# A fused two-block transformer kernel: 27 of the later modulation row chunks moved from TensorE to GpSimd, with one product with ones for each vector, and x loaded twice

## The chip, the cores and the metric

The kernel runs on one core of a Trainium2 chip. The metric is the device time of one execution in microseconds (us). Lower is better.

## What is computed

Two blocks follow each other on x (one sequence of 256 tokens, 2048 features, float32). The first has an RWKV-7 mixer beside a pooling mixer, the second has a short convolution beside banded attention, and both end in a gated convolutional feed-forward part. Only the modulation of the first block and what surrounds it matters here:

```python
c_act = jax.nn.silu(c)                      # c: 2048 numbers
mod = c_act @ w_ada[l] + b_ada[l]           # w_ada: 2048 x 12288
sh1, sc1, gt1, sh2, sc2, gt2 = jnp.split(mod[:, None, :], N_MOD, axis=-1)
h = _rmsnorm(x, norm1_g[l]) * (1.0 + sc1) + sh1
p = h @ w_in[l]
y_rwkv = _rwkv7_mixer(p[..., :N_RWKV_COLS], ...)   # a recurrence over 256 tokens, 16 heads
y_pool = _pool_mixer(p[..., N_RWKV_COLS:], ...)
mix = jnp.concatenate([y_rwkv, y_pool], axis=-1) @ w_out[l]
x = x + gt1 * mix
h = _rmsnorm(x, norm2_g[l]) * (1.0 + sc2) + sh2
x = x + gt2 * _conv_ffn(h, w_up[l], conv_w[l], conv_b[l], w_down[l])
```

`mod` is one row of six vectors of 2048 numbers. `w_ada` is 100 MB of weights that are each used once.

## The kernel before

Everything lies transposed: features on the 128 partitions, tokens on the free axis. Weights come as chunks of 128 x 2048 float32 (1 MB) through one ring `raw` of four places. All loads are issued by SyncE in one fixed order, `ORDER` (L77, L91). Before the load of place r, SyncE waits until the chunk in place r - 4 is free: a modulation chunk is free when TensorE has used it (`ada_used`), a weight chunk when VectorE has cut its second half (`lo_ready`, L537). SyncE handles its queue strictly in order.

A weight chunk is cut in two halves of 128 x 1024. ScalarE writes the high part (`whi`, L1278), VectorE the rest (`wlo`, L1734), and TensorE multiplies with both (L630, L631).

A modulation chunk is 128 rows of `w_ada` times one of the six vectors. There are 96, 16 for each vector. `ada_chunk` (L670) makes four matmuls of 512 columns with the column of silu(c) for these rows, repeated 32 times (`crep`), into the four quarters of one PSUM bank `ada` (L679). After 16 chunks ScalarE copies the bank to `ada_row` (`copy_ada`, L1338), TensorE turns it, and VectorE adds the bias.

The chunks of the first two vectors are used in the norm and the pooling projection. The 64 chunks of the last four vectors lie in the part that follows: an opening (L1077) and three segments (L1107). In the opening, TensorE projects the first group of heads; in segment s (1, 2, 3) it projects the next group while it does the recurrence of group s - 1. Each segment has 16 steps n. A step consists of quarter tiles of the projection (four pairs of L630 and L631), a step of the recurrence, and on even n two modulation chunks. The last segment (4) has no modulation and multiplies with `w_out` instead; its results are added to x.

The recurrence inverts small matrices in levels. For level 1 to 5 TensorE makes `z_step` (L830; matmuls L846), VectorE copies (L1960), TensorE makes `t_step` (L859, L865), and ScalarE copies the result (L1406). GpSimd prepares the masked matrix `bm` of each level (`levels`, L2489; the instruction is L2498), one or two levels ahead of TensorE. Apart from that GpSimd is idle in these segments. At the end of each segment comes `bonus_step` (L968).

x (128 x 16 x 256, 2 MB) is loaded at the start. It is read by the two norms of the first block until about 155 us, and not again until the last segment's `residual_tile` (L2113).

Of the kernel before, what the change touches and what calls it, by code (L numbers as in the profile page):

```python
# [17 lines left out]
ALU = mybir.AluOpType  # L18
# [8 lines left out]
KT = DM // P  # L27
# [9 lines left out]
CHUNK = 2048  # L37
# [3 lines left out]
NGROUP = 4  # L41
# [31 lines left out]

OPEN_ADA = {2: 2, 3: 1, 4: 2, 5: 1, 6: 2, 7: 2, 8: 1, 9: 2, 10: 1, 11: 2}


def raw_order():  # L77
    order = [("ada", a) for a in range(KT)] + [("w", 0)]
    a = KT
    for m in range(8):  # L80
        if m < 7:
            order.append(("w", m + 1))
        for _ in range(POOL_ADA.get(2 * m, 0) + POOL_ADA.get(2 * m + 1, 0)):
            order.append(("ada", a))
            a += 1
    w = FIRST_CHUNK["wkv"]
    order += [("w", c) for c in range(FIRST_CHUNK["lora"], w + 2)]
    c = w + 2
    for s in range(NGROUP):
        for n in range(2 if s == 0 else 0, 12 if s == 0 else 16):  # L90
            if n in ((2, 4, 6, 8, 10) if s == 0 else (0, 3, 5, 8, 11, 13)):  # L91
                order.append(("w", c))
                c += 1
            for _ in range(OPEN_ADA[n] if s == 0 else 2 - 2 * (n % 2)):
                order.append(("ada", a))
                a += 1
    return order + [("w", m) for m in range(c, N_WEIGHT_CHUNKS)]


ORDER = raw_order()  # L100
N_RAW = len(ORDER)
PLACE = [r for r, (what, _) in enumerate(ORDER) if what == "w"]
# [29 lines left out]
def source(r):  # L132

    what, n = ORDER[r]
    return KT * VECTORS[n // KT] + n % KT if what == "ada" else weights_at(n)

# [108 lines left out]
def blocks_program(nc, stream, x_in, param_in, lora_in, pool_w_in, pool_inv_in, res_in, wkv_in, att_in, out):  # L245
    with ExitStack() as ctx:
# [102 lines left out]
        catt = att("catt", [P, N_CATT])  # L349

        gated2 = layout(places["gates"])("gated2", [P, KT, 2, T], F32R)

# [47 lines left out]
        rows_ready, rows_wide, twice_rows, twice_wide = sem("rows_ready"), sem("rows_wide"), sem("twice_rows"), sem("twice_wide")  # L400
        pe_held, pool_held = sem("pe_held"), sem("pool_held")
        root_kept, gate_kept = sem("root_kept"), sem("gate_kept")
        lora_act, lora_mm, lora_out = sem("lora_act"), sem("lora_mm"), sem("lora_out")
# [119 lines left out]
        def _(sp):  # L523
# [30 lines left out]
            def load_halves(r, n):  # L554
# [41 lines left out]
            ends = [PLACE[FIRST_CHUNK[phase]] for phase in later][1:] + [N_RAW]  # L596
            for phase, end in zip(later, ends):
# [16 lines left out]
        def _(pe):  # L614
# [55 lines left out]
            def ada_chunk(n):  # L670

                r, kt = ADA_PLACE[n], n % KT
                pe.wait_ge(raw_full[r % RING], 16 * (r // RING + 1))
                if kt == 0 and n // KT:

                    pe.wait_ge(ada_copied, n // KT)
# [400 lines left out]
            def opening():  # L1077
                pe.wait_ge(tile_sum, FIRST_TILE["lora"])
                ada = iter(range(ADA0, ADA0 + KT))
                for n in range(OPEN_FIRST, SEG_HALVES):  # L1080
# [10 lines left out]
                    if 6 <= n <= 9:  # L1091
                        lora_gate(n - 6)
                    for _ in range(OPEN_ADA[n]):
                        ada_chunk(next(ada))
                    if n == 6:
# [6 lines left out]
                    if n == 11:  # L1102
                        pool_step(2)
                        pool_step(3)
                        bonus_step(0)

            def segment(s):  # L1107
                last = s == SEGMENTS - 1
                for n in range(16):
                    steps = recurrence_step(n, s - 1)  # L1110
                    for part in range(2):
                        if last:
                            next(steps)
                        for q in quarters(s, n, part):
                            quarter(s, q)
                        if part == 1 and n % 2 == 0 and not last:
                            for a in (n, n + 1):
                                ada_chunk(ADA0 + KT * s + a)
                        if not last:
# [7 lines left out]
                    if n == 7 and not last:  # L1127
                        kk_step(s)
                    if n == 15 and not last:
                        bonus_step(s)  # L1130

# [136 lines left out]
        def _(act):  # L1268
            def cut_hi(k, i=0, dh=0, dr=0):

                if isinstance(i, int) and k + dh * i >= 2 * N_WEIGHT_CHUNKS:
                    return
                r = PLACE[k // 2] if k // 2 < N_WEIGHT_CHUNKS else N_RAW + k // 2 - N_WEIGHT_CHUNKS
                act.wait_ge(raw_full[r % RING], 16 * (r // RING + 1) + 16 * (dr // RING) * i)
# [63 lines left out]
            def copy_ada(n):  # L1338

                act.wait_ge(ada_used, KT * (n + 1))  # L1340
                if n:
# [382 lines left out]
        def _(dve):  # L1724
            link, enter, leave = make_chain(dve, dve_chain)

            def cut_lo(k, i=0, dh=0, dr=0):

                if isinstance(i, int) and k + dh * i >= 2 * N_WEIGHT_CHUNKS:
                    return  # L1730
                r = PLACE[k // 2] if k // 2 < N_WEIGHT_CHUNKS else N_RAW + k // 2 - N_WEIGHT_CHUNKS

# [380 lines left out]
            def residual_tile(phase, j, i, scale):  # L2113

                t = FIRST_TILE[phase] + j
                dst = one(x, j + 4 * i)

                def add(half):
# [321 lines left out]
        def _(pool):  # L2440
# [47 lines left out]

            def levels(g):  # L2489
# [9 lines left out]

            levels(0)  # L2500
            with pool.Fori(1, NGROUP) as i:
                levels(i)

# [154 lines left out]
```

## Time and profile before

| | |
|---|---|
| time, median of 3 runs | 2683.87 us (2682.71 to 2685.06) |
| profiled execution, first to last instruction | 2692.6 us |
| TensorE matmul busy | 2619.7 us, 97% |
| TensorE weight load busy | 2180.2 us, 81% |
| VectorE busy | 1835.1 us, 68% |
| ScalarE busy | 1277.2 us, 47% |
| GpSimd busy | 147.2 us, 5% |
| DMA | 554.86 MB, 206 GB/s on average |

The profile gives for the profiled execution only its span; it lies 8.7 us above the median of the timed runs. PE is TensorE's matmul, PEld its weight load, DVE VectorE, ACT ScalarE, POOL GpSimd, SP SyncE; L679 is line 679 of the kernel. The opening lies at about 160 to 235 us of the span, the three segments at 233 to 312, 312 to 391 and 391 to 471 us.

### The profile page before, as it was taken

Reading aid. Unit: us, or ns where it says so; the run is one execution under the profiler, and the core shown is the slowest. Engines: PE = TensorE matmul, PEld = TensorE weight load, DVE = VectorE, ACT = ScalarE, POOL = GpSimd, SP = SyncE. Lnnn points to the kernel's source line nnn. Section 1 sums busy time; section 2 is a strip of 40 time slices with the busy share of each in tenths; the row PEclk is TensorE's granted clock in tenths of the full one; section 3 lists DMA queues with packets and bytes.
Section 4 is the critical chain, followed back from the end, with each engine's and each line's share of the span. In section 5 each row is a group of like instructions: output and inputs, shape, how many; then the busy total and the mean of one; then the engine's idle time right before and its main releaser. Section 6 shows DMA issues by size and latency. Waiting matters only on the chain.

```text
span 2692.6 us, 48237 instructions
## 1 busy us (share of the span) xinstructions
PE 2619.7 (97%) x17788; PEld 2180.2 (81%) x17788; DVE 1835.1 (68%) x2686; ACT 1277.2 (47%) x1800; POOL 147.2 (5%) x148
## 2 busy tenths in 40 slices
PE   5999999999999999999999999999999999999998
PEld 1566666788888888888888888888888888888887
DVE  1465665778777777655567777777688888886554
ACT  2253334355555555444433356555555555554443
POOL 1311100120000000010000000000100000000000
PEclk8999999999999999999999999999999999999999
DMA  9977777345555555555545544455555555555553
GB/s 370 390 294 278 287 308 296 113 151 190 184 184 184 185 186 187 203 196 210 211 172 188 179 164 157 156 175 197 185 186 192 188 187 187 188 189 208 206 194 138
DMA packets 86806, 554.86 MB, mean 206 GB/s; under 512 B 8496, under 2 KB 8624, under 8 KB 24496
## 3 DMA queue, kind: packets, MB, share of 16 engines
q1 hardware_dynamic: 86272, 551.78, 55.9%
q8 instruction: 74, 1.21, 0.2%
q10 hardware_dynamic: 432, 1.64, 0.2%
q14 instruction: 28, 0.23, 0.0%
HBM read 551.29 MB, written 2.10 MB: 206 GB/s over the span
## 4 chain that ended last, share of the span: by engine, by line
PE 86%; DVE 4%; issue 4%; DMA 4%; ACT 1%; DVEq 0%; POOL 0%; SPq 0%; ACTq 0%; POOLq 0%
PE bank L630 38%; PE bank L631 19%; PE banks L630 15%; PE banks L631 8%; DMA raw<-in_stream_dram 4%; PE bank L679 2%; DVE wlo L1734 2%; DVE yb L2408 0%; DVE yb L2411 0%; PE banks L846 0%; PE banks L1211 0%; PE banks L1231 0%; ACT whi L1278 0%; PE banks L865 0%; PE banks L1220 0%
## 5 line engine op out<-in xcount | busy, mean ns | idle before, releaser
L1734 DVE TENSOR_TENSOR wlo<-raw,whi 128x1024 fp32r<-128x1024 f32 x846 | 1028.2, 1225 | 216.1 <-ACT whi L1278 211.6
L1278 ACT ACTIVATE whi<-raw 128x1024 fp32r<-128x1024 f32 x846 | 877.5, 1051 | 460.7 <-PE bank L631 327.9
L630 PE MATMUL bank<-act,whi 128*128 128x512 f32 x2928 | 1052.6, 402 | 4.4 <-ACT mix L1467 3.0
L631 PE MATMUL bank<-act,wlo 128*128 128x256 f32 x2928 | 821.1, 280 | 0.0
L630 PEld LDWEIGHTS bank<-act,whi 128*128 128x128 f32 x2928 | 549.8, 188 | 158.2 <-issue 20.1
L630 PE MATMUL banks<-act,whi 128*128 128x512 f32 x1792 | 636.6, 398 | 7.9 <-DVE act L1784 6.8
L631 PEld LDWEIGHTS bank<-act,wlo 128*128 128x128 f32 x2928 | 553.6, 189 | 0.7 <-issue 0.5
L631 PE MATMUL banks<-act,wlo 128*128 128x256 f32 x1792 | 504.6, 282 | 0.0
L630 PE MATMUL bank<-ff,whi 128*128 128x512 f32 x1408 | 493.3, 393 | 1.2 <-DVE wlo L1734 1.2
L630 PEld LDWEIGHTS banks<-act,whi 128*128 128x128 f32 x1792 | 338.7, 189 | 94.3 <-issue 12.7
L631 PE MATMUL bank<-ff,wlo 128*128 128x256 f32 x1408 | 392.9, 279 | 0.0
L631 PEld LDWEIGHTS banks<-act,wlo 128*128 128x128 f32 x1792 | 341.3, 190 | 0.0
L630 PEld LDWEIGHTS bank<-ff,whi 128*128 128x128 f32 x1408 | 263.8, 187 | 64.9 <-DVE wlo L1734 1.9
L1562 ACT ACTIVATE yb<-joined,par 128x256 f32<-128x256 f32 x176 | 105.7, 602 | 352.8 <-DVE joined L1754 181.5
L631 PEld LDWEIGHTS bank<-ff,wlo 128*128 128x128 f32 x1408 | 263.8, 187 | 0.0
L2168 DVE SCALAR_TENSOR_TENSOR yb<-joined,par,yb 128x255 f32<-128x255 f32 x352 | 169.3, 481 | 24.5 <-DVE yb L2168 0.9
L2458 POOL TENSOR_TENSOR ssq<-ssq,ft 128x256 f32<-128x256 f32 x75 | 71.4, 952 | 1368.0 <-ACT ft L1548 1349.0
L679 PE MATMUL bank<-raw,crep 128*32 128x512 f32 x768 | 106.7, 658 | 29.0 <-DMA raw<-in_stream_dram 29.0
L630 PE MATMUL bank<-gated,whi 128*128 128x512 f32 x256 | 89.7, 393 | 0.4 <-DVE yb L2408 0.4
L679 PEld LDWEIGHTS bank<-raw,crep 128*32 128x32 f32 x768 | 19.1, 113 | 79.7 <-DMA raw<-in_stream_dram 45.1
L1548 ACT ACTIVATE ft<-x 128x256 f32 (+1 forms) x64 | 26.5, 414 | 105.8 <-DVE x L2120 86.2
L2120 DVE TENSOR_TENSOR x<-bank,x 128x256 f32 (+1 forms) x64 | 27.2, 424 | 70.0 <-PE bank L631 68.9
(277 smaller groups left out, 1898.2 us busy)
## 6 DMA issues: line engine op xcount, KB each, us to landing
raw<-in_stream_dram SPq DMA_DIRECT2D x519, 1024.0 KB, 4.8
x<-in_x_dram SPq DMA_DIRECT2D x1, 2048.0 KB, 13.8
lora_w<-in_lora_dram SPq DMA_DIRECT2D x1, 1536.0 KB, 14.3
pool_w<-in_pool_w_dram SPq DMA_DIRECT2D x1, 1024.0 KB, 12.1
out_dram<-x SPq DMA_DIRECT2D x2, 512.0 KB, 2.8
out_dram<-x ACTq DMA_DIRECT2D x2, 512.0 KB, 3.0
catt<-in_att_dram ACTq DMA_DIRECT2D x1, 576.0 KB, 3.4
par<-in_params_dram SPq DMA_DIRECT2D x1, 541.5 KB, 3.7
```

Source lines behind the costliest of these rows:

```text
L630: nc.tensor.matmul(tile_bank(t), wh, flat(pair[:, kt]), start=starts and n == 0, stop=False)
L631: mm = nc.tensor.matmul(small_half(t), wl, pair[:, kt, 0], start=False, stop=stops and last)
L679: mm = nc.tensor.matmul(ada[32 * g:32 * g + 32, :], crep[:, kt], src[:, 512 * g:512 * g + 512], start=kt == 0, stop=kt == KT - 1, tile_pos ...
L1278: nc.scalar.activation(whi[:, k % RING], raw[:, r % RING, 8 * (k % 2):8 * (k % 2) + 8], ACT.Copy)\
L1548: nc.scalar.activation(ft[:, j % 2], one(x, j + 4 * i), ACT.Square).then_inc(sq_ready, 1)
L1562: nc.scalar.activation(yb[:, j], joined[:, j % 2], ACT.Identity, scale=pcol(conv, 3 * j + tap + 12 * i), bias=pcol(bias, j + 4 * i)).then_ ...
L1734: nc.vector.tensor_tensor(wlo[:, k % RING], raw[:, r % RING, 8 * (k % 2):8 * (k % 2) + 8], whi[:, k % RING].bitcast(F32), ALU.subtract).th ...
L2120: return nc.vector.tensor_tensor(dst, half, dst, ALU.add)
L2168: ins = nc.vector.scalar_tensor_tensor(out=yb[:, j, dst], in0=joined[:, j % 2, src], scalar=pcol(conv, 3 * j + tap + 12 * i), in1=yb[:, j, ...
L2458: nc.gpsimd.tensor_tensor(ssq[:], ssq[:], ft[:, q], ALU.add).then_inc(ssq_ready, 1)
```

## The change

TensorE keeps 10, 9, 9 and 9 of the 16 chunks of the last four vectors. The other 6, 7, 7 and 7 (27 chunks) no longer go through the ring. They are loaded as 54 pieces of 128 x 1024 (0.5 MB) into two buffers in the first half of x. GpSimd multiplies each piece with its column of silu(c) and adds it to a sum of 128 x 2048 in the second half of x (the two pieces of a vector's first chunk are written to the sum without an addition). When all pieces of a vector are added, TensorE adds the sum over the partitions to the bank with four matmuls with ones (`ada_sum`), placed just ahead of `bonus_step` at the end of the opening and of each segment. The loads of the pieces stand in SyncE's queue behind loads of the ring (`pieces_behind`), and each waits until GpSimd has added the piece before the last. GpSimd adds one piece ahead of each of the levels 2 to 5 and the others behind the levels. x is loaded again in two halves once its place is free. The main parts of the diff:

```diff
-OPEN_ADA = {2: 2, 3: 1, 4: 2, 5: 1, 6: 2, 7: 2, 8: 1, 9: 2, 10: 1, 11: 2}
+OPEN_ADA = {2: 2, 3: 1, 4: 1, 5: 1, 6: 1, 7: 1, 8: 1, 9: 1, 10: 1}
+
+SEGMENT_ADA = {0: 2, 2: 1, 6: 1, 8: 2, 10: 2, 12: 1}
+
+PE_ROWS = (16, 16, 10, 9, 9, 9)
+ADA = [(v, kt) for v in range(6) for kt in range(PE_ROWS[v])]
+ADA_END = [sum(PE_ROWS[:v + 1]) for v in range(6)]
+
+PIECE = 1024
+PIECES = [(v, kt, g) for v in range(2, 6) for kt in range(PE_ROWS[v], KT) for g in range(CHUNK // PIECE)]
+PIECE_END = {v: CHUNK // PIECE * sum(KT - n for n in PE_ROWS[2:v + 1]) for v in range(2, 6)}
+PIECE_RING = 2
+
+LEVEL_PIECES = 1
...
-            for _ in range(OPEN_ADA[n] if s == 0 else 2 - 2 * (n % 2)):
+            for _ in range((OPEN_ADA if s == 0 else SEGMENT_ADA).get(n, 0)):
...
+def pieces_behind():
+
+    starts = [ADA_PLACE[ADA_END[v - 1]] + 3 for v in range(2, 6)] + [PLACE[FIRST_CHUNK["woutp"]] + 3]
+    behind = {}
+    for v in range(2, 6):
+        first, last = PIECE_END.get(v - 1, 0), PIECE_END[v]
+        lo, hi = starts[v - 2], starts[v - 1]
+        for r in range(lo, hi):
+            behind[r] = range(first + (last - first) * (r - lo) // (hi - lo), first + (last - first) * (r + 1 - lo) // (hi - lo))
+    return behind
...
+            def load_piece(i):
+
+                v, kt, g = PIECES[i]
+                if i == 0:
+
+                    sp.wait_ge(a_ready, 16 * (FILLS.index("h1") + 1))
+                if i >= PIECE_RING:
+                    sp.wait_ge(piece_added, i - PIECE_RING + 1)
+                src = stream[KT * VECTORS[v] + kt, :, PIECE * g:PIECE * (g + 1)]
+                sp.dma_start(pieces[:, i % PIECE_RING], src).then_inc(piece_full[i % PIECE_RING], 16)
...
+                for i in PIECES_BEHIND.get(r, ()):
+                    load_piece(i)
+                if what == "w" and n == FIRST_CHUNK["woutp"] + 3:
+                    sp.wait_ge(piece_added, len(PIECES))
+                    sp.dma_start(x[:, 0:8], x_in[:, 0:8]).then_inc(x_again[0], 16)
+                    sp.wait_ge(ada_summed, 4)
+                    sp.dma_start(x[:, 8:16], x_in[:, 8:16]).then_inc(x_again[1], 16)
...
+            def ada_sum(v):
+
+                pe.wait_ge(piece_added, PIECE_END[v])
+                for g in range(4):
+                    mm = nc.tensor.matmul(ada[32 * g:32 * g + 32, :], ones[:, 0:32], ada_acc[:, 512 * g:512 * (g + 1)],
+                                          start=False, stop=True, tile_position=(0, 32 * g))
+                mm.then_inc(ada_summed, 1)
...
+            def add_piece(i):
+
+                v, kt, g = PIECES[i]
+                pool.wait_ge(piece_full[i % PIECE_RING], 16 * (i // PIECE_RING + 1))
+                acc, piece = ada_acc[:, PIECE * g:PIECE * (g + 1)], pieces[:, i % PIECE_RING]
+                if kt == PE_ROWS[v]:
+
+                    if v > 2:
+                        pool.wait_ge(ada_summed, v - 2)
+                    nc.gpsimd.tensor_scalar(acc, piece, crep[:, kt, 0:1], None, ALU.mult).then_inc(piece_added, 1)
+                else:
+                    nc.gpsimd.tensor_scalar(piece, piece, crep[:, kt, 0:1], None, ALU.mult).then_inc(piece_scaled, 1)
+                    pool.wait_ge(piece_scaled, i + 1 - CHUNK // PIECE * (v - 1))
+                    pool.wait_ge(piece_added, i + 1 - CHUNK // PIECE)
+                    nc.gpsimd.tensor_tensor(acc, acc, piece, ALU.add).then_inc(piece_added, 1)
...
                 for level in range(6):
+                    if behind is not None and level >= 2:
+                        for _ in range(LEVEL_PIECES):
+                            add_piece(next(behind))
```

With these tables the pieces stand in SyncE's queue as follows. In segments 1 and 2 the first two stand behind loads that become possible at n = 0, the third behind one that TensorE frees at n = 2, the next behind loads freed at n = 3, 5 and 6, and the last eight behind eight loads freed one after the other from n = 8 to n = 13. In segment 3 (the last vector) everything stands one place earlier, and seven are left from n = 8 on. In the opening the last two stand behind a load that VectorE frees with the last low part of the opening (L1734 at n = 11) and the load after it.

## Rows read from the trace of the kernel before

**Rows 1.** The page: span, and busy time, share and instructions of an engine.
```profile
span 2692.6 us, 48237 instructions
PE 2619.7 (97%) x17788; PEld 2180.2 (81%) x17788; DVE 1835.1 (68%) x2686; ACT 1277.2 (47%) x1800; POOL 147.2 (5%) x148
```

**Rows 2.** Stretches: us, busy PE, PEld, DVE, ACT, POOL, PEclk, DMA share, GB/s.
```profile
160.00:235.00 75.00, 68.38 (x464) 42.75 (x466) 34.61 (x49) 29.77 (x51) 1.09 (x1) 0.95 0.74 297
313.00:392.00 79.00, 76.44 (x1134) 53.90 (x1130) 47.60 (x84) 30.03 (x52) 8.67 (x6) 1.00 0.77 293
```

**Rows 3.** TensorE in order of time, segment 2: start, duration, instruction, count.
```profile
327.71 0.69 PE L846 MATMUL banks<-tinvt,bm 64*64 64x64 f32 x32
336.53 1.92 PE L679 MATMUL bank<-raw,crep 128*32 128x512 f32 x16
338.38 0.69 PE L846 MATMUL banks<-tinvt,bm 64*64 64x64 f32 x32
343.31 0.69 PE L846 MATMUL banks<-tinvt,bm 64*64 64x64 f32 x32
389.07 1.02 PE L968 MATMUL bank<-ft,res 128*128 128x512 f32 x2
```

**Rows 4.** GpSimd in order of time, the levels 2 to 5 of segment 2.
```profile
322.11 1.27 POOL L2498 TENSOR_TENSOR bm<-nb,cw 128x512 f32<-128x512 f32 x1 [2.00 <-DVE tinvt L1956]
325.99 1.56 POOL L2498 TENSOR_TENSOR bm<-nb,cw 128x512 f32<-128x512 f32 x1 [2.61 <-ACT tinvt L1406]
333.14 2.04 POOL L2498 TENSOR_TENSOR bm<-nb,cw 128x512 f32<-128x512 f32 x1 [5.58 <-ACT tinvt L1406]
336.87 1.29 POOL L2498 TENSOR_TENSOR bm<-nb,cw 128x512 f32<-128x512 f32 x1 [1.69 <-ACT tinvt L1406]
```

**Rows 5.** GpSimd in order of time: other instructions with one and two inputs.
```profile
152.85 0.61 POOL L2478 COPY pad_a<-mix 128x512 f32<-128x512 f32 x1 [31.95 <-DVE mix L1751]
153.54 1.04 POOL L2482 TENSOR_TENSOR pad_b<-pad_a 128x512 f32<-128x512 f32 x1
557.00 0.74 POOL L2458 TENSOR_TENSOR ssq<-ssq,ft 128x256 f32<-128x256 f32 x1 [58.32 <-ACT ft L1548]
```

**Rows 6.** VectorE, then GpSimd, in order of time around 103 us.
```profile
102.17 3.11 DVE L1734 TENSOR_TENSOR wlo<-raw,whi 128x1024 fp32r<-128x1024 f32 x2 [0.64 <-ACT whi L1278]
...
102.72 1.49 POOL L2478 COPY pad_a<-mix 128x512 f32<-128x512 f32 x1
104.29 1.90 POOL L2482 TENSOR_TENSOR pad_b<-pad_a 128x512 f32<-128x512 f32 x1
```

**Rows 7.** VectorE in order of time, segment 2 from step 8 on.
```profile
356.00 2.35 DVE L1734 TENSOR_TENSOR wlo<-raw,whi 128x1024 fp32r<-128x1024 f32 x2
371.43 0.69 DVE L1915 TENSOR_TENSOR bk<-yb,aa 128x512 f32<-128x512 f32 x1
373.09 2.35 DVE L1734 TENSOR_TENSOR wlo<-raw,whi 128x1024 fp32r<-128x1024 f32 x2
381.53 1.22 DVE L1734 TENSOR_TENSOR wlo<-raw,whi 128x1024 fp32r<-128x1024 f32 x1 [0.82 <-ACT whi L1278]
```

**Rows 8.** The page's DMA issues: count, KB each, us from issue to landing.
```profile
raw<-in_stream_dram SPq DMA_DIRECT2D x519, 1024.0 KB, 4.8
out_dram<-x SPq DMA_DIRECT2D x2, 512.0 KB, 2.8
```

**Rows 9.** Short stretches around TensorE's wait at 168 us, columns as in Rows 2.
```profile
168.00:172.00 4.00, 0.42 (x6) 0.21 (x8) 1.74 (x3) 3.23 (x8) 0.00 (x0) 1.00 1.01 426
172.00:176.00 4.00, 4.00 (x32) 1.06 (x24) 3.84 (x7) 3.54 (x9) 0.00 (x0) 0.57 0.86 363
```

**Rows 10.** VectorE, then TensorE, in order of time at the opening's end.
```profile
219.18 1.22 DVE L1734 TENSOR_TENSOR wlo<-raw,whi 128x1024 fp32r<-128x1024 f32 x1
...
226.26 1.02 PE L968 MATMUL bank<-ft,res 128*128 128x512 f32 x2
230.32 0.80 PE L630 MATMUL bank<-act,whi 128*128 128x512 f32 x1 [3.04 <-ACT mix L1467]
```

More of the change, by code:

```diff
@@ L134, in source @@
     what, n = ORDER[r]
-    return KT * VECTORS[n // KT] + n % KT if what == "ada" else weights_at(n)
+    return KT * VECTORS[ADA[n][0]] + ADA[n][1] if what == "ada" else weights_at(n)
+def pieces_behind():
[7 more added lines that the diff above has]
+    return behind
+PIECES_BEHIND = pieces_behind()
 TILES = {"pool": 8, "lora": 3, "wkv": 24, "woutp": 16, "wout": 16, "up1": 88, "down1": 16, "qkv": 12, "cvb": 24, "gates": 32, "ao": 32,
@@ L349, in blocks_program @@
         catt = att("catt", [P, N_CATT])
+        ada_acc = x[:, 8:16].rearrange("p k t -> p (k t)")
+        pieces = x[:, 0:8].rearrange("p k t -> p (k t)").rearrange("p (b n) -> p b n", b=PIECE_RING)
         gated2 = layout(places["gates"])("gated2", [P, KT, 2, T], F32R)
@@ L401, in blocks_program @@
         pe_held, pool_held = sem("pe_held"), sem("pool_held")
+        piece_full = [sem(f"piece_full{n}") for n in range(PIECE_RING)]
+        x_again = [sem("x_again_low"), sem("x_again_high")]
+        piece_scaled, piece_added, ada_summed = sem("piece_scaled"), sem("piece_added"), sem("ada_summed")
         root_kept, gate_kept = sem("root_kept"), sem("gate_kept")
@@ L595, in _ @@
             later = ["up1", "qkv", "up2"]
-            ends = [PLACE[FIRST_CHUNK[phase]] for phase in later][1:] + [N_RAW]
+            ends = [PLACE[FIRST_CHUNK[phase]] for phase in later][1:] + [N_RING]
             for phase, end in zip(later, ends):
@@ L670, in ada_chunk @@
             def ada_chunk(n):
-                r, kt = ADA_PLACE[n], n % KT
+                r, (v, kt) = ADA_PLACE[n], ADA[n]
                 pe.wait_ge(raw_full[r % RING], 16 * (r // RING + 1))
-                if kt == 0 and n // KT:
-                    pe.wait_ge(ada_copied, n // KT)
+                if kt == 0 and v:
+                    pe.wait_ge(ada_copied, v)
                 src = raw[:, r % RING].rearrange("p k n -> p (k n)")
@@ L1078, in opening @@
                 pe.wait_ge(tile_sum, FIRST_TILE["lora"])
-                ada = iter(range(ADA0, ADA0 + KT))
+                chunks = iter(range(ADA_END[1], ADA_END[2]))
                 for n in range(OPEN_FIRST, SEG_HALVES):
@@ L1092, in opening @@
                         lora_gate(n - 6)
-                    for _ in range(OPEN_ADA[n]):
-                        ada_chunk(next(ada))
+                    for _ in range(OPEN_ADA.get(n, 0)):
+                        ada_chunk(next(chunks))
                     if n == 6:
@@ L1108, in segment @@
                 last = s == SEGMENTS - 1
+                chunks = iter(range(ADA_END[s + 1], ADA_END[s + 2])) if not last else None
                 for n in range(16):
@@ L1115, in segment @@
                             quarter(s, q)
-                        if part == 1 and n % 2 == 0 and not last:
-                            for a in (n, n + 1):
-                                ada_chunk(ADA0 + KT * s + a)
+                        if part == 1 and not last:
+                            for _ in range(SEGMENT_ADA.get(n, 0)):
+                                ada_chunk(next(chunks))
                         if not last:
@@ L1272, in cut_hi @@
                     return
-                r = PLACE[k // 2] if k // 2 < N_WEIGHT_CHUNKS else N_RAW + k // 2 - N_WEIGHT_CHUNKS
+                r = PLACE[k // 2] if k // 2 < N_WEIGHT_CHUNKS else N_RING + k // 2 - N_WEIGHT_CHUNKS
                 act.wait_ge(raw_full[r % RING], 16 * (r // RING + 1) + 16 * (dr // RING) * i)
@@ L1730, in cut_lo @@
                     return
-                r = PLACE[k // 2] if k // 2 < N_WEIGHT_CHUNKS else N_RAW + k // 2 - N_WEIGHT_CHUNKS
+                r = PLACE[k // 2] if k // 2 < N_WEIGHT_CHUNKS else N_RING + k // 2 - N_WEIGHT_CHUNKS
                 dve.wait_ge(hi_ready, k + 1 + dh * i)
@@ L2116, in residual_tile @@
                 dst = one(x, j + 4 * i)
+                if phase == "woutp" and j in (0, 8):
+                    dve.wait_ge(x_again[j // 8], 16)
                 def add(half):
@@ L2498, in levels @@
                     nc.gpsimd.tensor_tensor(bm[:, level % 2], nb[:, :, 0], mask, ALU.mult).then_inc(level_ready, 1)
-            levels(0)
-            with pool.Fori(1, NGROUP) as i:
-                levels(i)
+            for i in range(PIECE_END[2]):
+                add_piece(i)
+            for g in range(NGROUP):
+                behind = iter(range(PIECE_END[g + 2], PIECE_END[g + 3])) if g < NGROUP - 1 else None
+                levels(g, behind)
+                for i in behind or ():
+                    add_piece(i)
             for name in ("x1", "x2", "x4", "x5"):
```

12 lines of the change are left out of this document (9 added, 3 removed).

## The prediction

> **What bounds the kernel now.** I read the page first: TensorE's matmuls are busy 97% of the span and GpSimd 5% [rows 1], so an instruction taken from TensorE looks like a plain gain and GpSimd looks free. The stretches come next: in the opening TensorE is busy 68.4 of 75 us, in segment 2 76.4 of 79 us, and the DMA engines 74 to 77% [rows 2]. Segments 1 and 3 look alike. So these stretches are bound by TensorE. Then I read the engines in order of time within one segment, since the question is not how much GpSimd works but when each of its results is due. I count in the times of segment 2 in the old trace (it begins at 312.3), as if the changed segment began there too.
>
> **What is taken away.** Two modulation chunks, with what follows them starting 1.85 us later (336.53 to 338.38), cost 0.925 us each on TensorE [rows 3]. 27 of them are 25.0 us: 5.5 in the opening, 6.5 in each segment. Each product with ones has the same four shapes: 0.93, four times 3.7 us. A chunk between two steps of the recurrence also covers a wait. At n = 4 level 4 needs ScalarE's copy, which came 0.3 us after the step before; at n = 14 the spread of the variance is due about 0.8 us before its columns are ready. I put 1.1 us per segment on TensorE for that (between 0 and 2). If everything else were hidden, the change would save 25.0 - 3.7 - 3.3 = 18 us.
>
> **What a piece costs on GpSimd.** No 128 x 1024 instruction of GpSimd is in the trace. One input: a copy of 512 elements takes 0.61 us [rows 5], so twice the length is 1.05 to 1.2; at the rate of a multiplication with two inputs (1.27 for 512 [rows 4]) it would be 2.3. Two inputs: 0.74 for 256 [rows 5] and 1.27 for 512 [rows 4] give 2.1 ns an element, 2.35 us for 1024; by the row with 1.04 [rows 5] it would be 1.9. I take the copy and the 2.1 ns, since scaling reads one tensor and the addition reads two different ones: 1.05 + 2.35 + two gaps of 0.08 = 3.55 us a piece. The ends are 3.0 and 4.8.
>
> **GpSimd and VectorE hold each other up.** From 102.17 to 106.19 us VectorE ran two low parts and GpSimd a copy and an addition [rows 6]. Alone these take 2.35, 0.61 and 1.04 us [rows 5, 7], together 4.00; the stretch is 4.02 long. So each ran only while the other stood. I therefore add VectorE's work that reads SBUF twice to GpSimd's where the two meet. From step 8 to step 14 that is four low parts (4.8 us), three products for bk (2.1), and a handful of instructions of 0.2 to 0.7 us (4.1), some 11 us (the long ones are in [rows 7]). The Trainium skill ("SBUF — State Buffer", Who interferes with whom) states it for this case: VectorE with two SBUF inputs and GpSimd reading SBUF contend, and "the other fully blocks"; rows 6 agree. If the stretch at 102 us were chance and the two shared without loss, my sum would be 2695 instead of 2732 (second rival).
>
> **When the pieces arrive.** SyncE's queue is in order, and the new loads stand behind loads that wait for TensorE or VectorE. A load lands 4.8 us after its issue, one of half the size after 2.8 [rows 8]; queued, 1 MB takes 1.05/426 GB/s = 2.46 us [rows 9], a piece 1.23. So a piece lands 4.8 + 1.2 + 0.4 (issue) = 6.4 us after what frees the load ahead of it.
> Levels: the third piece stands behind a load freed at n = 2, at 326.7. It lands at about 332.6, VectorE's low parts (to 334.0, less 0.9) hold it, it is added at 336.6, and level 4's mask takes 1.3 more: 337.9. TensorE comes to level 4 at 338.38 - 0.93 - 1.85 + 0.3 = 335.9 [rows 3]; it waits 2. The fourth piece is freed by the low parts of n = 3 (333 to 334) and lands at 339.5; with a low part in between, the mask for level 5 (1.69 us idle before it now [rows 4]) is ready at 345.4, due at 335.9 + 2 + 4.9 = 342.8: another 2.4. So 4.4 us in segments 1 and 2 (between 1 and 8); in segment 3 the pieces stand one place earlier and I count 0.
> The end of the segment: the low parts of step 8 end at 358.35 [rows 7], less 3.7 + 0.3 for chunks gone and the wait exposed, plus 4.4: 359.4. From here eight pieces must be loaded and added. The first lands at 365.8. The loads keep pace (1.5 MB per piece is 3.7 us of DMA at most), so GpSimd sets it: 8 x 3.55 = 28.4, and 11 us of VectorE: 405.2. The product with ones takes 0.9, so `bonus_step`, at 389.07 now [rows 3], begins at 406.1: **17 us later** in segments 1 and 2 each. TensorE would have come at about 389.07 - 6.5 + 1.1 + 4.4 = 388 and stands for 17 us.
> Segment 3: seven pieces from 354.95 + 6.4 = 361.4: 24.9 + 11 gives 397.2, `bonus_step` at 398.1: **9 us later**.
> Opening: the last low part ends at 220.4 [rows 10]. TensorE's 5.5 us less and GpSimd's 2 to 4 us in between leave about 218. Behind it 3 MB are queued (load, piece, load, piece): landing at 218.3 + 4.8 + 4.9 = 228. The last piece is added at about 232.5, product and bonus take it to 234.5; the first matmul of the segment, which now waits 3.04 us for ScalarE and starts at 230.32 [rows 10], starts near 235: **5 us later** (between 0 and 8).
>
> **What else moves.** When TensorE waits 3.6 us its clock falls from 2.4 to 1.2 GHz for some 3 us [rows 9]: about 1.5 us after each long stand; the opening has one already, so I leave these 4 us to the range. The second load of x is 2 MB, 4.9 us of DMA. SyncE waits in front of it for the last sum, behind it stand the chunks of the last segment from the fifth on, due some 30 us later: nothing. x is first needed about 5 us into the last segment and was issued before its start: nothing, 5 us if that cover went. ScalarE's `copy_ada` waits for the sum, but it stands behind its other work of the segment: nothing. VectorE's instructions that wait for GpSimd in steps 8 to 14 delay TensorE less than it stands anyway.
>
> **Sum.** 2 x 17 + 9 + 5 = 48 us. The profile's span is 2692.6, the changed one's would be 2741; on the median, 2683.9 + 48 = **2732 us**.
>
> **The rivals.** (1) Forecast, 0.60: GpSimd's backlog from step 8 on, drawn out by VectorE, sets the end of each segment. Its own range is 2708 to 2755 (3 us less or more per late group of pieces).
> (2) VectorE and GpSimd rarely meet, 0.15. Then 365.8 + 28.4 + 0.9 = 395.1, +6 us in segments 1 and 2; 361.4 + 24.9 + 0.9 = 387.2, -2 in segment 3; opening +2: 2695. For it: in the old segment GpSimd's instructions are mostly 1.27 to 1.29 long beside a busy VectorE [rows 4]. Against it: two of the four stand longer, 1.56 and 2.04.
> (3) Faster, 0.14: the pieces are short and early enough that TensorE never waits for a sum. It decides at one place, step 8 to 15: from the first landing (about 361 without the waits at the levels) to TensorE's arrival at 383.7 are 22.7 us, 2.8 us for each of eight pieces. With less than that the sums cost nothing and the saving of 18 us stands: 2666. For it: GpSimd is idle now and 512 elements can be added in 1.04. Against it: even with the low ends, 1.05 + 1.9, a piece is 3.0.
> (4) Scaling by a number from memory runs at the rate of two inputs, 4.8 us a piece, 0.11: 365.8 + 38.4 + 12 + 0.9 is +28 in segments 1 and 2, +17 in segment 3, +9 in the opening, and 4 more at the levels of the first two: 2774.
> That the work isn't moved is excluded by the tables: 37 chunks of 64 remain on TensorE.
>
> **How the numbers follow.** Measurements of this kernel can tell 0.2%, 5.4 us. Faster by more: rival 3 without its upper edge, 0.12. Within: the edges of rivals 2 and 3, 0.08. Slower: 0.80. The range leaves out rival 3 and most of rival 4's upper half: 2681 to 2770.
>
> **What would show it.** In the changed profile: GpSimd's scale about 1.1 and its addition about 2.4 us, both longer where low parts run beside them; GpSimd without a pause from about step 9 to the end of each segment; TensorE idle 10 to 17 us ahead of the ones product, ended by GpSimd, and idle 2 us ahead of L846 at the levels 4 and 5 of segments 1 and 2; the clock low after it; the three segments about 96, 96 and 88 us instead of 79. Wrong it would be if a piece takes under 2.8 us, if SyncE's issues don't wait for GpSimd, or if TensorE's idle time ahead of the sum ends with a DMA.

## The result and the profile after

The changed kernel takes 2782.95 us (2778.25 to 2790.72), the kernel before beside it 2684.47 (2682.71 to 2694.43): a ratio of 1.0353 with a 95% interval of 1.0331 to 1.0376, 98.5 us slower. Forecast were 48 us. Its profiled span is 2779.4 us. The profiled execution of before was the slowest of its four, and its part behind the last `bonus_step` below was long (2224 us, 2211 in the changed kernel), so below I compare the places inside the segments, where the two traces can be laid on each other.

The page of the changed kernel: span and engines, the granted clock in 40 slices, two of the costliest groups, the DMA issues.
```profile
span 2779.4 us, 48032 instructions
PE 2611.0 (94%) x17604; PEld 2186.8 (79%) x17604; DVE 1893.2 (68%) x2686; ACT 1277.7 (46%) x1800; POOL 437.5 (16%) x248
...
PEclk8998898999999999999999999999999999999999
...
L2569 POOL TENSOR_SCALAR x<-x,crep 128x1024 f32<-128x1024 f32 x46 | 152.6, 3318 | 34.5 <-DMA x<-in_stream_dram 34.4
L2572 POOL TENSOR_TENSOR x<-x 128x1024 f32<-128x1024 f32 x46 | 113.2, 2461 | 3.8
...
raw<-in_stream_dram SPq DMA_DIRECT2D x492, 1024.0 KB, 4.8
x<-in_stream_dram SPq DMA_DIRECT2D x54, 512.0 KB, 5.8
```
Against [rows 1]: TensorE has 184 instructions less but only 8.7 us less busy time, where 25.0 less 3.7 was counted; GpSimd has 290 us more. The scale takes 3.3 us on average, the addition 2.5.

`bonus_step`, the end of the opening and of each segment, in the order of TensorE in the trace of before (the other two are in [rows 10] and [rows 3]):
```profile
309.88 1.02 PE L968 MATMUL bank<-ft,res 128*128 128x512 f32 x2
...
468.26 1.02 PE L968 MATMUL bank<-ft,res 128*128 128x512 f32 x2
```
The same in the trace of the changed kernel:
```profile
245.85 1.90 PE L1030 MATMUL bank<-ft,res 128*128 128x512 f32 x2
...
355.51 1.22 PE L1030 MATMUL bank<-ft,res 128*128 128x512 f32 x1
...
465.37 2.08 PE L1030 MATMUL bank<-ft,res 128*128 128x512 f32 x2
...
568.39 2.08 PE L1030 MATMUL bank<-ft,res 128*128 128x512 f32 x2
```
The opening ends 19.6 us later (5 forecast). The segments take 109.7, 109.9 and 103.0 us instead of 83.6, 79.2 and 79.2: 26.0, 30.7 and 23.8 more (17, 17 and 9 forecast). By 568 us the whole loss is there, 100.1 us.

TensorE's waits between 150 and 600 us in the changed kernel (line, waited for: us in total, times, longest):
```profile
PE bank L741 <- POOL x L2572: 66.2, 4, 22.2
PE banks L908 <- POOL bm L2586: 12.6, 7, 4.4
```
Four stands ahead of the ones product, 15.1, 18.6, 22.2 and 10.2 us, each ended by GpSimd's addition. The mechanism of the forecast is there; its size is not. What GpSimd does meanwhile, in order of time, segment 1 of the changed kernel from the first to the last of the eight late pieces:
```profile
306.90 2.84 POOL L2569 TENSOR_SCALAR x<-x,crep 128x1024 f32<-128x1024 f32 x1 [4.60 <-DMA x<-in_stream_dram]
309.83 2.39 POOL L2572 TENSOR_TENSOR x<-x 128x1024 f32<-128x1024 f32 x1
...
348.33 2.84 POOL L2569 TENSOR_SCALAR x<-x,crep 128x1024 f32<-128x1024 f32 x1
351.26 2.34 POOL L2572 TENSOR_TENSOR x<-x 128x1024 f32<-128x1024 f32 x1
```
It has one pause of 0.70 us in 46.7. An undisturbed piece is 2.84 + 2.34 and one gap of less than 0.1 between them, 5.25 us from start to start (343.09 to 348.33), and not 3.55: **the scale is 2.84 us, not 1.05.**

### The profile page after: what moved, and what is told of

It is laid out like the page before. It is cut to its first block, busy times and chain, and to the rows that moved or that the text cites. A ratio compares the mean times of both kernels' runs of the same rounds, so it can differ in the third digit from the quotient of the medians.

```text
span 2779.4 us, 48032 instructions
## 1 busy us (share of the span) xinstructions
PE 2611.0 (94%) x17604; PEld 2186.8 (79%) x17604; DVE 1893.2 (68%) x2686; ACT 1277.7 (46%) x1800; POOL 437.5 (16%) x248
## 4 chain that ended last, share of the span: by engine, by line
PE 78%; POOL 10%; issue 5%; DMA 3%; DVE 3%; ACT 1%; DVEq 0%; SPq 0%; ACTq 0%; POOLq 0%
PE bank L684 35%; PE bank L685 18%; PE banks L684 15%; PE banks L685 8%; POOL x L2569 5%; POOL x L2572 3%; DMA raw<-in_stream_dram 3%; DVE wlo L1801 1%; POOL bm L2586 1%; PE bank L733 1%; DVE yb L2477 0%; DVE yb L2480 0%; DMA x<-in_stream_dram 0%; POOL x L2567 0%; PE banks L1276 0%
## 5 line engine op out<-in xcount | busy, mean ns | idle before, releaser
L1801 DVE TENSOR_TENSOR wlo<-raw,whi 128x1024 fp32r<-128x1024 f32 x846 | 1044.9, 1244 | 267.0 <-ACT whi L1343 262.4
L684 PEld LDWEIGHTS bank<-act,whi 128*128 128x128 f32 x2928 | 553.4, 189 | 150.6 <-issue 23.8
L2569 POOL TENSOR_SCALAR x<-x,crep 128x1024 f32<-128x1024 f32 x46 | 152.6, 3318 | 34.5 <-DMA x<-in_stream_dram 34.4
L2524 POOL TENSOR_TENSOR wssq<-wssq,yb 128x256 f32<-128x256 f32 x15 | 11.2, 749 | 705.6 <-ACT ft L1615 705.6
L733 PE MATMUL bank<-raw,crep 128*32 128x512 f32 x552 | 83.3, 692 | 33.8 <-DMA raw<-in_stream_dram 33.8
L2572 POOL TENSOR_TENSOR x<-x 128x1024 f32<-128x1024 f32 x46 | 113.2, 2461 | 3.8
```

The costliest lines, as they stand in the source:

```text
L684: nc.tensor.matmul(tile_bank(t), wh, flat(pair[:, kt]), start=starts and n == 0, stop=False)
L1801: nc.vector.tensor_tensor(wlo[:, k % RING], raw[:, r % RING, 8 * (k % 2):8 * (k % 2) + 8], whi[:, k % RING].bitcast(F32), ALU.subtract).th ...
L2524: link(nc.gpsimd.tensor_tensor(wssq[:], wssq[:], yb[:, q], ALU.add))
L2569: nc.gpsimd.tensor_scalar(piece, piece, crep[:, kt, 0:1], None, ALU.mult).then_inc(piece_scaled, 1)
L2572: nc.gpsimd.tensor_tensor(acc, acc, piece, ALU.add).then_inc(piece_added, 1)
```

## The experiments

The reasons to be told apart: (A) the time of a piece on GpSimd sets the end of each segment; (B) the two engines' holding each other up does; (C) the loads do, by their number or by their place in SyncE's queue. Each time is given against the kernel before on the same chip.

**The saving alone.** `none`: `PIECES = []`, no wait and no instruction on GpSimd; the 27 chunks are left out of the sum, the four products with ones stay.
```diff
-PIECES = [(v, kt, g) for v in range(2, 6) for kt in range(PE_ROWS[v], KT) for g in range(CHUNK // PIECE)]
+PIECES = []
```


> The 27 chunks are left out altogether: no pieces, no work on GpSimd, so the last four vectors lack these rows. The four products with ones stay, without their wait, and so does the second load of x. My theory: TensorE is rid of 27 x 0.925 = 25.0 us, keeps 3.7 us for the four products, and 1.1 us of waits comes out in each segment: 18 us less than before, 2666 us. Rival: the chunks mostly covered waits of the recurrence, and little comes back: 8 us less at most, 2676 or more. Second rival: the opening also loses its wait of 3.0 us at its end, 21 us or more: 2663 or less.


Measured: 2674.5 us, ratio 0.9936 (0.9910 to 0.9961), 17 us faster. The saving of 18 us was right, and it is what the idea can bring at 27 chunks if nothing else costs time.

**A shorter piece, without the scale.** `add_only`: the pieces are added unscaled.
```diff
-                    nc.gpsimd.tensor_scalar(piece, piece, crep[:, kt, 0:1], None, ALU.mult).then_inc(piece_scaled, 1)
-                    pool.wait_ge(piece_scaled, i + 1 - CHUNK // PIECE * (v - 1))
```


> The scaling of the pieces is left out, so the sums are of unscaled rows (only each vector's first chunk is scaled). A piece should cost GpSimd 2.38 + 0.08 = 2.46 us instead of 5.4. If GpSimd's time per piece sets the end of a segment: from step 8 on eight pieces take 20 + 3 us instead of 47, the sums come about when TensorE does, bonus_step to bonus_step takes 78 to 79 us in segments 1 and 2 and 75 in segment 3, the opening ends 2 us later than before: 2680 us, 2672 to 2690. If the place of the loads in SyncE's queue set it, the sums would stay late and the time over 2720. If the sharing of SBUF with VectorE set it, an addition beside VectorE's low parts would take over 3.5 us and the time lie between, at 2700 to 2720.


Measured: 2735.9 us, 1.0164 (1.0140 to 1.0188), 44 us slower. So 2.84 us less a piece give back half of the loss, and a piece of some 2.5 us, under the 2.8 us that rival 3 asked for, still loses. None of the three forecasts fits: the time lies above 2720, but the sums are hardly late. TensorE waits for them 14.7 us in all, 10.0 of it in the opening, and the segments still take 96.6, 102.0 and 92.6 us from `bonus_step` to `bonus_step`. Something besides GpSimd's own time costs: B or C.

**The scale as a product of two tensors.** `scale_tt`: the column is repeated along the row as a second input.
```diff
-                    nc.gpsimd.tensor_scalar(piece, piece, crep[:, kt, 0:1], None, ALU.mult).then_inc(piece_scaled, 1)
+                    nc.gpsimd.tensor_tensor(piece, piece, crep[:, kt, 0:1].to_broadcast([P, PIECE]), ALU.mult).then_inc(piece_scaled, 1)
```


> The scaling is a product of two tensors, the second the column repeated over 1024 elements, instead of a product with a scalar from memory. If the scalar form runs at the rate of two inputs or slower because of its kind, this one takes 2.35 to 2.45 us instead of 2.85 (the masks of the levels, also with a repeated operand, take 1.27 for 512), a piece 4.9 instead of 5.4, and some 31 late pieces give 14 us back: 2769. If both forms cost the same, no change: 2783.


Groups of GpSimd's instructions in this kernel (mean ns behind the busy time):
```profile
L2572 POOL TENSOR_TENSOR x<-x 128x1024 f32<-128x1024 f32 x46 | 123.7, 2688 | 3.6
L2569 POOL TENSOR_TENSOR x<-x,crep 128x1024 f32<-128x1024 f32 x46 | 98.5, 2141 | 79.8 <-DMA x<-in_stream_dram 79.7
```
An undisturbed product, in order of time:
```profile
334.30 1.90 POOL L2569 TENSOR_TENSOR x<-x,crep 128x1024 f32<-128x1024 f32 x1 [1.96 <-DMA x<-in_stream_dram]
```
The multiplication with two inputs is faster, 2.14 us on average against 3.32 and 1.90 undisturbed against 2.84, yet the one execution took 2783.9 us, as long as the change (span 2782.1 against 2779.4). It was run once, so small differences can't be read from it; the 14 us forecast didn't appear. The time won per piece was lost again elsewhere: TensorE waits only 26.1 us for the sums instead of 66.2, but longer for VectorE's results, and GpSimd waits 79.7 us for pieces instead of 34.4. The views shown with `after_scale_twice` below say what does it.

**Loads and waits without GpSimd's time.** `tiny27`: all 54 pieces are loaded and waited for as in the change, but GpSimd touches 32 columns of each, in one instruction; the sum is left incomplete.
```diff
...
-                    nc.gpsimd.tensor_tensor(acc, acc, piece, ALU.add).then_inc(piece_added, 1)
+                    nc.gpsimd.tensor_scalar(acc[:, 0:32], piece[:, 0:32], crep[:, kt, 0:1], None, ALU.mult).then_inc(piece_added, 1)
```
(the scale of a piece goes, and the first pieces of a vector are cut to 32 columns in the same way)


> All 54 pieces are loaded in the changed kernel's order and all waits stay, but GpSimd multiplies only the first 32 columns of a piece and adds nothing (the sums are not the reference's). What is left is the order of SyncE's queue and the loads. Theory A, now: the order alone costs little; GpSimd's time and its additions cost the rest. The sums wait for the last landing, 1 to 2 us a segment, and the time is that of leaving the chunks out (17 us less than before) plus 2 to 6: 11 to 15 us less than before. Theory B, the order itself starves the ring or holds the sums back: no less than before, or more.


Measured: 2695.1 us, 1.0029 (1.0007 to 1.0051), 8 us slower, 25 us above `none`. With GpSimd almost idle TensorE still stands 20.2 us for the sums. GpSimd in order of time, segment 1 of `tiny27`:
```profile
296.55 0.36 POOL L2570 TENSOR_SCALAR x<-x,crep 128x32 f32<-128x32 f32 x1 [2.34 <-DMA x<-in_stream_dram]
300.50 0.36 POOL L2570 TENSOR_SCALAR x<-x,crep 128x32 f32<-128x32 f32 x1 [3.59 <-DMA x<-in_stream_dram]
304.25 0.36 POOL L2570 TENSOR_SCALAR x<-x,crep 128x32 f32<-128x32 f32 x1 [3.38 <-DMA x<-in_stream_dram]
308.40 0.36 POOL L2570 TENSOR_SCALAR x<-x,crep 128x32 f32<-128x32 f32 x1 [3.80 <-DMA x<-in_stream_dram]
312.10 0.36 POOL L2570 TENSOR_SCALAR x<-x,crep 128x32 f32<-128x32 f32 x1 [3.33 <-DMA x<-in_stream_dram]
```
A piece arrives every 3.7 to 4.2 us. The stretch of 27 us around them (columns as in [rows 2]) shows why:
```profile
285.00:312.00 27.00, 19.33 (x191) 13.97 (x188) 17.09 (x30) 7.70 (x12) 3.23 (x6) 0.97 0.92 378
```
The DMA engines are busy 92% of it. Every piece comes with a load of 1 MB in this part of the segment, 1.57 MB at 378 GB/s is 4.2 us, and eight of them are 30 us and more. TensorE has used up its work before that: it is busy 19.3 of 27 us. This is C: with the loads in this order no piece can come faster than one in about 3.9 us, however fast GpSimd is.

**One instruction a piece.** `scale_only`: the scale writes to the accumulator and nothing is added, so that the sum holds the last piece alone.
```diff
-                    nc.gpsimd.tensor_tensor(acc, acc, piece, ALU.add).then_inc(piece_added, 1)
+                    nc.gpsimd.tensor_scalar(acc, piece, crep[:, kt, 0:1], None, ALU.mult).then_inc(piece_added, 1)
```
(and the first instruction of a piece goes)


> As with the additions alone, but each piece is one product with a scalar, 2.85 us with one input, and nothing is added. GpSimd works longer for each piece than with the additions alone (2.93 instead of 2.46 us), but VectorE's low parts run unhindered beside it. If holding VectorE back is what cost 44 us with the additions alone, this one is far below it in spite of the longer instruction: the sums wait about 3 us a segment and the clock falls once in each, 0 to 12 us more than before. If GpSimd's time per piece is what counts, it costs more than the additions alone: over 45 us more than before.


Measured: 2727.8 us, 1.0142 (1.0093 to 1.0191), 38 us slower; TensorE waits 41.1 us for the sums and 11.3 for the masks. The time lies between the two forecasts (0 to 12 us, and over 45). The full piece of 5.25 us adds another 57 us. The scale is the longer of the two instructions, and alone it costs no more than the addition alone: the intervals of the two ratios overlap. The two lose the time in different places. With the scale TensorE stands for the sums, 41.1 us against 14.7; with the addition it stands more for results of VectorE in the recurrence (`us` 7.6 us against 2.5, `zmat` 6.4 against 2.9, `rs` 4.8 against 1.7).

**Both instructions as scales.** `after_scale_twice`: the whole change with the addition replaced by a second scale into the accumulator (the sum is left out).
```diff
-                    nc.gpsimd.tensor_tensor(acc, acc, piece, ALU.add).then_inc(piece_added, 1)
+                    nc.gpsimd.tensor_scalar(acc, piece, crep[:, kt, 0:1], None, ALU.mult).then_inc(piece_added, 1)
```


> The changed kernel with the addition of each piece replaced by a second product with a scalar: 5.9 us a piece instead of 5.4, but no instruction with two inputs except the masks. If GpSimd's time sets the end of the segments, VectorE's release changes little: eight late pieces take 47 us as before with their waits for VectorE: 95 to 110 us more than before. If the hold on VectorE were a cause of its own in the full version, it would fall to 75 us or less in spite of the longer pieces.


Measured: 2794.3 us, 1.0393 (1.0359 to 1.0427), 105 us slower. If B set the end, this kernel would have gained, to 75 us or less. It didn't: the intervals of this ratio and of the change's overlap, and TensorE's stands for the sums grow from 66.2 to 87.7 us. So in the change with 27 chunks it is A that sets the end. What B adds to it isn't measured apart, since here a scale 0.5 us longer took the addition's place.

What B is, in three short views. VectorE, then GpSimd, around 424 us in the changed kernel:
```profile
406.43 2.35 DVE L1801 TENSOR_TENSOR wlo<-raw,whi 128x1024 fp32r<-128x1024 f32 x2
...
424.22 4.21 DVE L1801 TENSOR_TENSOR wlo<-raw,whi 128x1024 fp32r<-128x1024 f32 x2
```
```profile
404.64 2.84 POOL L2569 TENSOR_SCALAR x<-x,crep 128x1024 f32<-128x1024 f32 x1
407.57 3.45 POOL L2572 TENSOR_TENSOR x<-x 128x1024 f32<-128x1024 f32 x1
...
423.80 2.40 POOL L2572 TENSOR_TENSOR x<-x 128x1024 f32<-128x1024 f32 x1
426.19 4.86 POOL L2569 TENSOR_SCALAR x<-x,crep 128x1024 f32<-128x1024 f32 x1
```
The two low parts that start at 424.22, inside an addition, take 4.21 us: 2.35 from its end at 426.20 is 428.55, and they end at 428.43, so they stood until then. The two that start at 406.43, inside a scale with 1.05 us to go, take their bare 2.35 and hold the addition up. The same in `after_scale_twice`, VectorE, then GpSimd:
```profile
434.01 2.36 DVE L1801 TENSOR_TENSOR wlo<-raw,whi 128x1024 fp32r<-128x1024 f32 x2 [1.65 <-ACT whi L1343]
```
```profile
432.37 2.85 POOL L2569 TENSOR_SCALAR x<-x,crep 128x1024 f32<-128x1024 f32 x1
435.31 3.95 POOL L2572 TENSOR_SCALAR x<-x,crep 128x1024 f32<-128x1024 f32 x1
```
VectorE starts beside a scale that runs until 435.22 and isn't held, and the scale that starts at 435.31 is stretched by the 1.06 us that VectorE still needs. Over the whole traces, a low part that starts inside one of GpSimd's scales takes 1.28 us in the changed kernel (19 cases), one that starts inside an addition 2.24 (13 cases). **A low part that is running holds up either form that starts beside it; GpSimd's addition holds up a low part that starts inside it, its scale by a column doesn't.** Nor is the scale at 404.64 longer for the low parts that start inside it. That is where `scale_tt` loses what its shorter scale won: both of its forms hold VectorE, and a low part that starts inside one of them takes 2.66 us (25 cases). From 306 to 356 us VectorE is busy 40.6 us of 50 there, 26.6 in the changed kernel.

**Three chunks a vector.** `few3`: 12 chunks on GpSimd instead of 27, six pieces a segment instead of 14, each load behind a place of the ring that is freed at a step given by hand, and `LEVEL_PIECES` 0 instead of 1.
```diff
-PE_ROWS = (16, 16, 10, 9, 9, 9)
+PE_ROWS = (16, 16, 13, 13, 13, 13)
...
-LEVEL_PIECES = 1
+LEVEL_PIECES = 0
...
+DUE = ((3, 3, 5, 6, 7, 8), (0, 0, 5, 6, 8, 8))
```


> Only 3 chunks of each of the last four vectors go to GpSimd (12 chunks, 24 pieces), no piece stands ahead of a level, and the loads stand behind earlier places of the queue: in a segment two at n = 0, then n = 5, 6, 8, 8. GpSimd needs six pieces, two of 2.9 and four of 5.4 us. If the late sums are the whole loss, they now come before TensorE and only the saving is left: 12 x 0.925 = 11.1 less 3.7 for the products and 1 for waits that come out, 6 us less than before: 2678. If holding up VectorE costs TensorE time by itself, 2 us a segment: 2684 to 2688. If SyncE standing in front of a piece starves the ring: over 2695.


Measured: 2701.6 us, 1.0035 (1.0007 to 1.0064), 9 us slower. No wait for a sum is among TensorE's longer ones any more, and yet the saving doesn't appear. `few3_scale_twice` replaces the addition by a second scale, as above:


> 12 chunks on GpSimd as before, but the addition of each piece is replaced by a second product with a scalar (one input, 2.85 us instead of 2.4). If the additions' hold on VectorE is what turned the expected 6 us less into 9 us more, this one is 3 to 6 us faster than before. If it is any work of GpSimd, or the sums' waits, it is as slow as with the additions, 9 us more than before, or slower.


Measured: 1.0004 (0.9984 to 1.0025), 1 us slower, although its piece is longer, 6.2 us against 5.5. That is neither of the two forecasts. And `tiny3` lets GpSimd touch 32 columns of each piece:


> 12 chunks, loaded as pieces in the same order, GpSimd multiplies 32 columns of each and adds nothing. This is the floor of the version with 12 chunks: 11.1 us saved, less 3.7 for the four products, less 1 to 2 for waits that come out: 5 to 7 us less than before. If even this is not faster than before, the order of the loads or the products with ones cost it.


Measured: 0.9981 (0.9961 to 1.0001), 5 us faster, just within the noise. TensorE's longest group of waits between 150 and 600 us in `few3`, and the same line in `few3_scale_twice`:
```profile
PE banks L990 <- DVE rs L2044: 7.0, 3, 2.6
```
```profile
PE banks L990 <- DVE rs L2044: 1.9, 3, 1.2
```
When no backlog hides it, B shows in the traces: the additions delay VectorE's steps of the recurrence, and the last `bonus_step` of the segments comes at 485.92 us in `few3`, at 472.32 in `few3_scale_twice` and at 469.85 in `tiny3`. By the ratios the two kernels lie 8 us apart, but their intervals overlap, so that size is not shown. Even with GpSimd's work gone, three chunks a vector win only about 5 us, 0.2%.

**Other places for the loads.** If the late bunching is what costs in `tiny27`, earlier places should help: `tiny27_early` puts the loads of a segment behind places freed at the steps 0, 0, 2, 3, 5, 5, 6, 6 and six times 8, those of the opening at 3, 3, 4, 4 and so on to 8, 8. `add_early` and `after_early` are `add_only` and the change with the same table.
```diff
+DUE = ((3, 3, 4, 4, 5, 5, 6, 6, 7, 7, 8, 8), (0, 0, 2, 3, 5, 5, 6, 6, 8, 8, 8, 8, 8, 8))
```


> As the run with 32 columns of each of the 54 pieces, but the loads of the pieces stand behind earlier places of SyncE's queue: in a segment at n = 0, 0, 2, 3, 5, 5, 6, 6 and six at 8, in the opening two at each of n = 3 to 8, all from 3 to 8. In the run before, the eight pieces from step 8 on and the eight 1 MB loads between them were 12 MB, 30 us of DMA, where TensorE needs 23 us to the sum: the sums waited 2 to 6.6 us. If the crowding of the loads is what cost that run 25 us against leaving the chunks out, this one is at 8 to 14 us less than before. If the order costs through SyncE standing in front of pieces, it is as slow or slower, 5 us more than before or worse.

> The additions alone (no scaling), with the earlier places of the loads. It was 44 us slower than before with the places of the change; its sums waited 15 us in all. If late pieces cause most of it, this one comes down to 10 to 20 us more than before. If the additions' hold on VectorE and the falls of the clock cause it, it stays at 30 to 44 us more.

> The changed kernel in full (scaling and addition), with the earlier places of the loads. GpSimd's work in a segment is 2 x 2.9 + 12 x 5.4 = 70.6 us for the pieces, 8.7 for the masks and 4 of waiting for VectorE, 83 us against the old segment's 79. So even with every piece in time GpSimd sets the length of the segments, at 88 to 95 us instead of 103 to 110: 50 to 75 us more than before. If the places don't matter for it: 94 to 98 us more.


Measured: 1.0107 (1.0067 to 1.0146), 1.0263 (1.0232 to 1.0293) and 1.0464 (1.0428 to 1.0501): 29, 71 and 125 us slower, all three worse than with the places of the change by 21 to 30 us, and clear of noise. `add_early` and `after_early` meet neither of their forecasts. I had looked at DMA alone and not at who issues it. SyncE's queue in `tiny27_early`, in order of time:
```profile
279.29 0.33 SPq L584 DMA_DIRECT2D raw<-in_stream_dram  x1
279.66 14.67 SPq L620 DMA_DIRECT2D x<-in_stream_dram  x6
294.37 2.74 SPq L584 DMA_DIRECT2D raw<-in_stream_dram  x4
```
Its six pieces behind one place need 14.67 us, since each waits for a place of the two, and four loads of the ring stand behind them. TensorE's longest wait in this kernel is then not for a sum:
```profile
PE banks L1014 <- DVE us L2049: 29.3, 3, 10.6
```
VectorE's `us` stands behind low parts whose weights have not come; in `after_early` the same wait is 70.2 us. Places between the two tables, or loads issued from another queue, were not tried; how much of the 25 us of `tiny27` can be had back stays open.

## Why the prediction was wrong

**The saving** was right: 18 us forecast, 17 measured (`none`).

**The piece** was the step that failed. I took a scale of 1024 elements at twice a copy of 512 [rows 5], 1.05 us, and gave 2.3 as the upper end, the rate of a multiplication with two inputs. It is 2.84, above both ends; the real multiplication with two inputs takes 1.90 undisturbed. With its gap the piece is 5.25 us and not 3.55, above the upper end of 4.8 too. The Trainium skill ("GPSIMD Engine Reference", 4.1 Engine selection) calls one-input work on GpSimd roughly line-rate; the copy of [rows 5] agrees, with 0.61 us for 512 elements, 1.2 ns each as in VectorE's low part (1.22 us for 1024), and the scale does not, with 2.8 ns each. The addition was right, 2.35 forecast, 2.34 measured.

**The holding up** was over-counted: 11 us a segment forecast. In segment 1 the eight pieces take 46.7 us, which is 8 times 5.25 and 4.7 more, and 0.70 of that is the pause; in segment 2 it is 6.1 more. The rule read from [rows 6] is true for the copy and the addition there, and the Trainium skill's ("SBUF — State Buffer", Who interferes with whom) for additions, beside which a low part takes 2.24 us; the words "the other fully blocks" stand there for VectorE's two-port modes, and that two SBUF inputs contend is a sentence of its own. But beside a running scale VectorE isn't held (1.28 us), and in the last 14 us or so of the backlog in segments 1 and 2, 4 in segment 3, VectorE has nothing left to do, since it waits for TensorE, which waits for GpSimd.

**Segment 2 by the forecast's own sum**, counted from its `bonus_step`: the first of the eight pieces starts at 59.9 us instead of landing at 55.9, the eight take 48.1 us (to the product with ones at 463.50) instead of 39.4, and from there to the next `bonus_step` it is 1.9 instead of 0.9: 109.9 against 96.2. The eight pieces themselves give 8.7 of the 13.7 us missed: 13.6 more for the piece, 4.9 less for the holding up. The other 5 are the later start and the product and `bonus_step` behind the stand. Segment 3 is the same with seven pieces (41.8 instead of 35.9), but its first one starts 7.8 us later than forecast: I had counted no backlog from the pieces before it, and GpSimd was still at them until 522.87, 1.8 us before the late ones.

**The opening** was forecast from its last two pieces. In truth GpSimd is behind from the third piece on: the last ten take from 183.69 to 243.94, 6.0 us each, with 3.8 us of pauses for loads in 60.3. The sum is waited for 15.1 us, and the opening ends 19.6 us later instead of 5.

**The levels** came out: stands of 4.35 and 1.08 us at the levels 4 and 5 of segment 2, 5.4 together, and 4.00 and 1.32 in segment 1; 4.4 were forecast (4.6 by the forecast's own figures, 337.9 less 335.9 and 345.4 less 342.8). For the masks of segment 3 none is above 0.4.

**The clock** I had left to the range. Stretches of the changed kernel: the stand ahead of the sum in segment 2, the 4 us behind it, and the stretch from 469.3 us on.
```profile
446.00:464.00 18.00, 0.50 (x4) 0.20 (x8) 3.09 (x2) 0.00 (x0) 17.20 (x7) 0.50 0.40 140
464.00:468.00 4.00, 4.00 (x13) 1.51 (x6) 0.87 (x1) 2.45 (x3) 0.00 (x0) 0.50 0.03 6
469.30:472.00 2.70, 2.70 (x71) 2.02 (x73) 1.37 (x3) 0.00 (x0) 0.00 (x0) 1.00 0.50 149
```
TensorE stands, the granted clock is at half, 1.2 GHz, and stays there after the work has come back at 463.50, until 469.3: 5.8 us. In the opening and the segments 1 and 3 it is 3.4, 3.0 and 5.2 us (back at full at 247.4, 356.7 and 571.7). About 1.5 us after each long stand were counted, and left out of the sum; the page's clock line dips in the slices of the stands. Over the segments 1 to 3 TensorE is busy 232.8 us in the changed kernel at a mean clock of 0.88, and 216.9 us with the same chunks on TensorE in `none`, at 0.96 to 1.00: 16 us more. A part of that lies in front of a stand for GpSimd and costs nothing; the first of the late pieces starts 4 us late partly by it, and I can't split that further.

**The loads "keep pace"** was wrong by itself, but had no effect on the forecast's sign: they allow a piece every 3.9 us, GpSimd needs 5.25. At the forecast's own 3.55 the loads would have set the pace, already by its 3.7 us of DMA per piece. It refutes rival 3: with these loads its threshold of 2.8 us a piece can't be reached by any GpSimd, as `tiny27` shows, and `add_only`, with an instruction under it, loses 44 us.

Put in order by the ratios (the change is 95 us by its ratio, 98.5 by the medians): -17 for the saving; +25 for the loads and their order (`tiny27`); +30 for one instruction of 2.9 us a piece (`scale_only`); +57 for the second (the change). Rival 4, which had the scale at the rate of two inputs and gave 2774, came nearest; it was right on the cause, a slow scale, though not by the rate of two inputs, and I had given it 0.11. It came near in part by luck, since it counted 12 us of holding up where 5 to 6 were. The price was the one thing that the trace of before did not hold, and the copy was too kind a neighbour. The multiplication is not what makes the scale slow, since `scale_tt` multiplies by the same column as a second tensor in 1.90 us. Whether the form with a scalar is slow by itself or by its operand from memory was not tried apart.

## What to carry to other kernels

Work given to an idle engine is paid for where its results are due: count the pieces behind the last free place of the loads, multiply by the time of the whole piece, and compare with what the bound engine still has to do. Where the price of the new instruction isn't in the trace, let the range reach beyond the neighbour that looks slowest, and take a neighbour with the same kind of operands. Before moving a load forward, look at what its queue would stand for, and at what stands behind it.

## What the runs showed of the hardware

- GpSimd's multiplication of 128 x 1024 fp32 elements by a column from memory takes 2.84 us undisturbed, slower than the same product with the column repeated as a second tensor (1.90) and than the addition (2.34).
- The holding up is one-sided for that form: a low part that starts inside it takes 1.28 us on average (1.22 alone), inside an addition 2.24, while a scale or an addition that starts beside a running low part is held up (4.86 us at 426.19, 3.45 at 407.57).
- After the four long stands TensorE's granted clock is still at half for 3.0 to 5.8 us of work. Over the whole kernel TensorE's busy time falls by 8.7 us, where it falls by 17.5 in `none`, which gives TensorE the same instructions but has no stands for GpSimd.
